# Prompt attention chunkwise inside the V projection, a sigmoid gate, and the sample's state update moved into the output projection

## The reference, cut to what matters

```python
b = cumsum(lf); dmat = b[t] - b[s] + ig[s], -inf where s > t
m = maximum(b + m0, max(dmat))
s = (q @ k.T) * exp(dmat - m)
num = s @ v + exp(b + m0 - m) * (q @ C0)
h = num / maximum(abs(den), exp(-m))
C1 = exp(b[-1] + m0 - m[-1]) * C0 + (a * k).T @ v
y = (rmsnorm(h) * g_head * sigmoid(o)) @ w_out
```

## Time and profile before

| | |
|---|---|
| median of 3 runs | 1549.89 us (1546.93 to 1554.04) |
| profiled execution | 1557.0 us |
| its span | 1554.3 us |
| TensorE busy in the span | 1436.3 us, 92% |
| VectorE, ScalarE, GpSimd busy | 48%, 26%, 35% |
| TensorE's mean granted clock | 0.932 of 2.4 GHz |

### The profile page before, as it was taken

How to read it: one execution, slowest core, us unless ns; L and a number is a source line. 1 busy time by engine, 2 the same in 40 slices (tenths; PEclk the granted TensorE clock), 3 DMA queues, 4 the chain that set the end, 5 groups by cost and what they waited for, 6 DMA issues and landing times.

```text
span 1554.3 us, 28123 instructions
## 1 busy us (share of the span) xinstructions
PE 1436.3 (92%) x11820; PEld 1379.3 (89%) x11820; DVE 744.6 (48%) x1062; ACT 401.9 (26%) x641; POOL 538.4 (35%) x282
## 2 busy tenths in 40 slices
PE   5798998779798998999999979999979999999996
PEld 4687996558798998998999979999979999999996
DVE  3621166547347324324315761495875264462673
ACT  2422221025223222222222223222232222222222
POOL 1223341125332332332334424443423444444430
PEclk8698998859898999999999979999979999999997
DMA  9566541270562563563463312232312333223312
GB/s 275 171 124 152 161 125 41 78 45 1 142 168 83 149 184 106 146 187 111 138 190 86 94 55 82 82 96 84 92 45 82 95 88 87 83 78 96 94 55 58
DMA packets 328027, 167.45 MB, mean 108 GB/s; under 512 B 16159, under 2 KB 326119, under 8 KB 327794
## 3 DMA queue, kind: packets, MB, share of 16 engines
q1 hardware_dynamic: 241426, 121.07, 29.9%
q10 hardware_dynamic: 86336, 44.77, 10.5%
q0 software_dynamic: 160, 0.07, 0.0%
HBM read 158.97 MB, written 6.91 MB: 107 GB/s over the span
## 4 chain that ended last, share of the span: by engine, by line
PE 66%; issue 14%; POOL 6%; DVE 6%; SPq 4%; DMA 1%; ACT 1%; ACTq 0%; POOLq 0%; DVEq 0%
PE G L1247 42%; PE G L1269 14%; POOL wl L664 6%; SPq L301 2%; PE B L1526 2%; PE G L1504 2%; PE B L1287 1%; PE B L1468 1%; DMA raw<-in_mlstm_w_in 1%; SPq L336 1%; PE B L1297 1%; DVE small_s L1201 1%; PE B L1233 1%; DVE yc L1200 1%; PE B L1496 1%
## 5 line engine op out<-in xcount | busy, mean ns | idle before, releaser
L664 POOL TENSOR_TENSOR wl<-raw,wh 128x1024 fp32r<-128x1024 f32 x192 | 479.8, 2502 | 770.0 <-ACT wh L401 769.9
L1247 PE MATMUL G<-Xh,wh 128*128 128x272 f32 x1536 | 326.1, 294 | 0.0
L1247 PE MATMUL G<-Xl,wh 128*128 128x272 f32 x1536 | 319.5, 289 | 0.0
L1247 PE MATMUL G<-Xh,wl 128*128 128x272 f32 x1536 | 317.8, 288 | 0.0
L408 ACT ACTIVATE stage<-G 128x544 f32<-128x544 f32 x168 | 105.0, 625 | 687.5 <-PE G L1247 543.1
L1247 PEld LDWEIGHTS G<-Xh,wh 128*128 128x128 f32 x1536 | 241.7, 190 | 14.3 <-issue 14.3
L401 ACT ACTIVATE wh<-raw 128x1024 fp32r<-128x1024 f32 x192 | 202.4, 1054 | 197.0 <-PE G L1269 72.6
L1247 PEld LDWEIGHTS G<-Xl,wh 128*128 128x128 f32 x1536 | 243.7, 190 | 0.0
L1247 PEld LDWEIGHTS G<-Xh,wl 128*128 128x128 f32 x1536 | 242.6, 190 | 0.0
L810 DVE SCALAR_TENSOR_TENSOR xT<-stage,modT,xT 128x512 f32<-128x512 f32 x80 | 75.5, 944 | 308.9 <-ACT stage L408 287.1
L1247 PE MATMUL G<-Hh,wh 128*128 128x272 f32 x864 | 180.3, 290 | 0.0
(11 more groups left out here) (238 smaller groups left out, 1580.5 us busy)
## 6 DMA issues: line engine op xcount, KB each, us to landing
aring<-in_ada_w ACTq DMA_DIRECT2D x80, 512.0 KB, 5.1
raw<-in_mlp_w_up SPq DMA_DIRECT2D x64, 512.0 KB, 4.1
raw<-in_mlp_w_down SPq DMA_DIRECT2D x64, 512.0 KB, 3.9
raw<-in_mlstm_w_in SPq DMA_DIRECT2D x24, 512.0 KB, 3.8
raw<-in_conv_w_in SPq DMA_DIRECT2D x24, 512.0 KB, 3.8
early<-in_ada_w SPq DMA_DIRECT2D x16, 512.0 KB, 7.4
raw<-in_mlstm_w_out SPq DMA_DIRECT2D x8, 512.0 KB, 6.6
raw<-in_conv_w_out SPq DMA_DIRECT2D x8, 512.0 KB, 3.9
```

The lines of the kernel that those rows point to most:

```text
L664: nc.gpsimd.tensor_tensor(wl[:, t % SLOTS], raw[:, t % RAWS], wh[:, t % SLOTS].bitcast(F32), ALU.subtract).then_inc(s_lo, 1)
L1247: last = mm(G[:, 2 * (g % 2) + hf, 0:HALF], w[:, s, k, :], x[:, k, hf * HALF:(hf + 1) * HALF], start=st, stop=en)
```

## The change

Prompt attention goes by chunks of 128 tokens. A head now has only the four diagonal blocks of scores, four key-value products, a state carried over the chunks by VectorE (`states`), and per chunk after the first a product of decayed queries with the state. Its steps stand between the contraction steps of the V tile after its own (`head`), and at the end of that tile (`head_product`); head 7 stands in O tile 0. The prompt's state falls out of the last chunk, and SP stores it during O. The samples' rows are spread by small products on TensorE in place of the way through DRAM. The V projection has no modulation pairs; each later projection of layer 0 takes the set of the one before, and the first MLP's last quarter takes the last set. The gate is ScalarE's Sigmoid. The samples' old-state products and attention stand within O tiles, their state update within output-projection tiles 2 to 5, with one VectorE instruction for each of 32. SP's order: three V weights, the sample's state, the other V weights and four of O, the prompt state's stores, the rest of O; then, after the samples' rows are done (`s_ys`), x and all weights of the output projection; then the sample state's stores; then the MLP's. The first MLP's loop makes two passes, and the first and last quarters are written out.

```diff
-STATE_TILE = 4
+STATE_TILE = 2
@@ SyncE @@
+unit(T_V, w_in, D, order=range(3))
...
-unit(T_V, w_in, D)
-unit(T_O, w_in, 2 * D)
-unit(T_WOUT, w_out, 0, order=range(3))
+unit(T_V, w_in, D, order=range(3, KT))
+unit(T_O, w_in, 2 * D, order=range(4))
+sp.wait_ge(s_st, H)
+for h2 in range(2):
+    mine = Cfin[DK * h2:DK * (h2 + 1), :, :]
...
+unit(T_O, w_in, 2 * D, order=range(4, KT))
+sp.wait_ge(s_ys, 1)
+sp.wait_ge(s_out, 16 * 4)
+for k in range(KT):
+    nc.sync.dma_start(xT[:, k, :], xspill[:, k * TOK:(k + 1) * TOK]).then_inc(s_back, 16)
+unit(T_WOUT, w_out, 0)
 sp.wait_ge(s_cud, 1)
...
-sp.wait_ge(s_y, H)
-sp.wait_ge(s_num, H)
-for k in range(KT):
-    nc.sync.dma_start(xT[:, k, :], xspill[:, k * TOK:(k + 1) * TOK]).then_inc(s_back, 16)
-unit(T_WOUT, w_out, 0, order=range(3, KT))
...
@@ ScalarE @@
+    for i in range(NJ):
+        c = slice(i * P, (i + 1) * P)
+        last = nc.scalar.activation(dexp[h % 2][:, c], B4[:, c], ACT.Exp, bias=tok[:, 0, i, h:h + 1])
+    last.then_inc(s_d, 1)
...
+for m in range(KT):
+    if m >= 1:
+        decays(m - 1)
+    hi(T_V + m + LEAD)
+    if m >= 2:
+        turned_out(m - 2)
+    to_v(T_V + m, G_V + m, None, 0, 0)
+    if m >= 1:
+        head_out(m - 1)
...
+to_gate = to_stage(ACT.Sigmoid)
...
+    hi(T_O + m + LEAD)
...
+    to_gate(T_O + m, G_O + m, None, 0, 0)
...
@@ GpSimd @@
+def mask(h):
+    pool.wait_ge(s_d, h + 1)
+    blocks = dexp[h % 2][:, :].rearrange("p (j c) -> p j c", j=NJ)
+    nc.gpsimd.affine_select(out=blocks, in_=blocks, compare_op=ALU.is_ge, fill=0.0, base=0,
+                            pattern=[[0, NJ], [1, P]], channel_multiplier=-1).then_inc(s_sel, 1)
+def head_power(h):
+    pool.wait_ge(s_sq, h + 1)
+    nc.gpsimd.tensor_tensor(stat[:, 3, :], stat[:, 2, :], mhalf[:, 0:NJ], ALU.pow).then_inc(s_rs, 1)
...
+for h in range(-1, H):
+    if h >= 1:
+        head_power(h - 1)
+    if h >= 0:
+        mask(h)
+    lo(T_V + LEAD + h + 1)
@@ VectorE @@
+def scaled_queries(a):
+    if a:
+        dve.wait_ge(s_pv, 2 * a)
+    V.tensor_copy(decs[:, :], B6[:, P - 1:SEQ - P:P])
+    V.tensor_tensor(qt[:, :], qT[:, a, P:SEQ], B6[:, 0:SEQ - P], ALU.mult).then_inc(s_qe, 1)
+def weights(h):
+    dve.wait_ge(s_s, h + 1)
+    dve.wait_ge(s_sel, h + 1)
+    V.scalar_tensor_tensor(dexp[h % 2][:, :], B5[:, :], KS, dexp[h % 2][:, :], ALU.mult, ALU.mult).then_inc(s_pr, 1)
+def states(h):
+    pr = slice(DK * (h % 2), DK * (h % 2) + DK)
+    dve.wait_ge(s_u, h + 1)
+    dve.wait_ge(s_qe, h // 2 + 1)
+    if h >= 2:
+        dve.wait_ge(s_pv, h - 1)
+    chain.link(V.tensor_copy(Sst[pr, 0, :], B7[pr, 0:DVA]))
+    for i in range(1, NJ - 1):
+        chain.link(V.scalar_tensor_tensor(Sst[pr, i, :], Sst[pr, i - 1, :], decs[pr, i - 1:i],
+                                          B7[pr, i * DVA:(i + 1) * DVA], ALU.mult, ALU.add))
+    V.scalar_tensor_tensor(Cfin[pr, h // 2, :], Sst[pr, NJ - 2, :], decs[pr, NJ - 2:NJ - 1], B6[pr, 0:DVA],
+                           ALU.mult, ALU.add).then_inc(s_st, 1)
...
+for h in range(H):
+    if h:
+        head_factor(h - 1)
+    values(h)
+    if h % 2 == 0:
+        scaled_queries(h // 2)
+    if h:
+        head_done(h - 1)
+    weights(h)
+    states(h)
...
+mixer_residual = residual(2, 1)
+for m in range(KT):
+    mixer_residual(m, G_WOUT + m, None, 0)
+    if STATE_TILE - 1 <= m < STATE_TILE - 1 + H // 2:
+        update_state(m - STATE_TILE + 1)
@@ TensorE @@
+def head(h):
+    a, pr = h // 2, slice(DK * (h % 2), DK * (h % 2) + DK)
+    def between(k):
+        if k == 0:
+            if h >= 2:
+                pe.wait_ge(s_hc, h - 1)
+            elif h == 0:
+                pe.wait_ge(s_ktd, 4)
+            mm(B4[:, :], sel[:, h, :], negMp[:, :], start=True, stop=True).then_inc(s_bc, 1)
+        if k == 1:
+            if h:
+                pe.wait_ge(s_pr, h)
+            else:
+                pe.wait_ge(s_sp, 1)
+            for i in range(NJ):
+                c = slice(i * P, (i + 1) * P)
+                last = mm(B5[:, c], kT[pr, a, c], qT[pr, a, c], start=True, stop=True)
+            last.then_inc(s_s, 1)
+        if k == 2:
+            pe.wait_ge(s_ev, G_V + h + 1)
+            if h:
+                pe.wait_ge(s_num, h)
+            st_ = stage[(G_V + h) % 2]
+            for jt in range(NJ):
+                turn(B7[:, jt * P:(jt + 1) * P], st_[:, col(jt * P):col(jt * P) + P], P)
+            last = turn(B6[0:NS, SEQ - P:SEQ], vs[(G_V + h) % 2][:, :], P)
+            if h % 2 == 0:
+                last = mm(B6[:, 0:SEQ - P], selp[:, a, :], erow[:, :], start=True, stop=True)
+            last.then_inc(s_vt, 1)
+        if k == 5:
+            pe.wait_ge(s_dr, G_V + h + 1)
+            pe.wait_ge(s_qe, a + 1)
+            for i in range(NJ):
+                out = B7[pr, i * DVA:(i + 1) * DVA] if i < NJ - 1 else B6[pr, 0:DVA]
+                last = mm(out, ktok[:, i, h * DK:(h + 1) * DK], vtok[:, i, h, :], start=True, stop=True,
+                          tile_position=(0, DK * (h % 2)))
+            last.then_inc(s_u, 1)
+        if k == 6 and h:
+            pe.wait_ge(s_d, h + 1)
+            turn_head(h - 1)
+    return between
+def head_product(h):
+    a, pr = h // 2, slice(DK * (h % 2), DK * (h % 2) + DK)
+    pe.wait_ge(s_pr, h + 1)
+    pe.wait_ge(s_st, h + 1)
+    for jt in range(NJ):
+        out = (B7, B6)[jt // 2][:, (jt % 2) * DVA:(jt % 2 + 1) * DVA]
+        last = mm(out, dexp[h % 2][:, jt * P:(jt + 1) * P], vtok[:, jt, h, :], start=True, stop=(jt == 0))
+        if jt:
+            last = mm(out, qt[pr, (jt - 1) * P:jt * P], Sst[pr, jt - 1, :], start=False, stop=True)
+    last.then_inc(s_pv, 1)
+for m in range(KT):
+    tile(T_V + m, G_V + m, Xh, Xl, None, 0, 0, head(m - 1) if m else before_heads)
+    if m:
+        head_product(m - 1)
...
+O_STEPS = {(1, 5): lambda: turn_head(H - 1), (3, 1): sample_numerators, (5, 1): sample_turned}
...
+for m in range(KT):
+    tile(T_O + m, G_O + m, Xh, Xl, None, 0, 0, gate_steps(m) if m else head(H - 1))
+    if m == 0:
+        head_product(H - 1)
+    if m == 1:
+        sample_scores()
+    if m == 2:
+        pe.wait_ge(s_hc, H)
+    if m in ADA_AFTER_O:
+        ada_pair(4 * 3 + ADA_AFTER_O[m])
+pe.wait_ge(s_ys, 1)
+ada_turn(3)
...
-            mm((B5, B7)[n % 2][:, 0:2 * DVA], kam[a % 2][:, b, :],
-               vtok_s[:, 2 * a:2 * a + 2, :].rearrange("p h e -> p (h e)"), start=True, stop=True).then_inc(s_cu, 1)
+            for h2 in range(2):
+                last = mm((B5, B7)[n % 2][DK * h2:DK * (h2 + 1), 0:DVA], kam[a % 2][:, b, DK * h2:DK * (h2 + 1)],
+                          vtok_s[:, 2 * a + h2, :], start=True, stop=True, tile_position=(0, DK * h2))
+            last.then_inc(s_cu, 1)
...
+mixed(T_WOUT, G_WOUT, 4, Yh, Yl, x_ready(X_Y), between=state_products)
...
-with pe.Fori(0, QUARTERS - 1) as j:
-    mixed(T_MLP0, G_MLP0, 6, Xh, Xl, MLP0_X, j, 16, 16, 2)
-    mixed(T_MLP0 + 8, G_MLP0 + 8, 7, Hh, Hl, drained(G_MLP0, j, 16), j, 16, 16, 2)
-unit(T_MLP0_LAST, G_MLP0_LAST, Xh, Xl, ready=MLP0_X)
+mixed(T_MLP0, G_MLP0, 5, Xh, Xl, MLP0_X)
+mixed(T_MLP0 + 8, G_MLP0 + 8, 6, Hh, Hl, drained(G_MLP0))
+with pe.Fori(0, QUARTERS - 2) as j:
+    mixed(T_MLP0L, G_MLP0L, 7, Xh, Xl, MLP0_X, j, 16, 16, 2)
+    mixed(T_MLP0L + 8, G_MLP0L + 8, 8, Hh, Hl, drained(G_MLP0L, j, 16), j, 16, 16, 2)
+mixed(T_MLP0_LAST, G_MLP0_LAST, 11, Xh, Xl, MLP0_X)
```

More of the change, by code:

```diff
@@ L534, in rows_sample, with maxima_out @@
                 nc.scalar.activation(sample(rows[2][:, :]), sample(rows[2][:, :]), ACT.Exp).then_inc(s_ra, 1)
[L536 to L540 removed]
+            def maxima_out():
                 nc.scalar.dma_start(outs[4][0, 0, :].rearrange("(h o) -> h o", o=1), rows[0][:, LAST_COL:LAST_COL + 1])\
@@ L1098, in head_norm, with norm_heads @@
                 V.tensor_scalar(st[2], st[4], 1.0 / DV, EPS, ALU.mult, ALU.add).then_inc(sq_sem, 1)
-                if meanwhile is not None:
-                    meanwhile()
+            def norm_heads(nm, npart, w, rs_n, hs_out, out_sem):
+                st = [stat[0:npart, i, 0:w] for i in range(5)]
                 dve.wait_ge(s_rs, rs_n)
@@ new lines, in _ @@
+            head_factor(H - 1)
+            head_done(H - 1)
+            gated(0)
+            dve.wait_ge(s_srs, 5)
+            chain.link(V.tensor_tensor(qe[:, :, :], qs[:, :, :], einter_s[:, :, :], ALU.mult))
+            for h2 in range(2):
+                pr = slice(DK * h2, DK * (h2 + 1))
+                for b in range(SB):
+                    last = V.tensor_copy(qbd[pr, :, b, NS * h2 + ST * b:NS * h2 + ST * (b + 1)], qe[pr, :, ST * b:ST * (b + 1)])
+            last.then_inc(s_sp, 1)
@@ new lines, in _ @@
+            gated(1)
+            dve.wait_ge(s_ssc, 1)
+            for h2 in range(2):
+                pick = lambda ap: ap.rearrange("p (a h) t -> p a h t", h=2)[:, :, h2, :]
+                last = V.scalar_tensor_tensor(
+                    pick(probs_s[:, :, :])[:, :, NS * h2:NS * (h2 + 1)],
```

(21 more changed lines are left out.)

676 lines of the change are left out of this document (289 added, 387 removed).

## The result

| | before | after |
|---|---|---|
| median of 4 runs | 1550.56 us (1546.93 to 1554.04) | 1574.27 us (1563.21 to 1587.37) |
| ratio after to before | | 1.0119, 95% interval 1.0082 to 1.0156 |
| profiled execution, span | 1557.0, 1554.3 us | 1565.4, 1563.8 us |
| mean granted clock | 0.932 | 0.932 |

One of the four runs of after, 1587.37 us, counts as slow and is left out of the ratio; the median of the other three is 1565.4 us.

The account below looks back on a forecast made before the run. Matmuls bound V, O and output projection; keys, gap and attention left TensorE idle. Terms -12.4 + 44.9 - 121.6 + 57.3 - 0.5 = -32.3 us, median 1549.9 to 1517.6; 8-in-10 range 1487 to 1546.

Parts of the forecast that it names:

- Step 1: Query and key tiles: stall behind the state's loads goes, half of 11.6 us idle kept; 62.4 against 74.8, -12.4 us.
- Step 2: V with seven heads: tile 0 at 12.2, seven tiles at 13.3; 105.3 against 60.4, +44.9 us.
- seven products at 0.243: End of each tile with a head: seven products on TensorE, 1.7 us of the head's 6.2 us.
- Rivals B and C: V tiles: B, heads' hand-over becomes the bound, 1567 us, chance 0.08; C, nothing of a head hides, 1550, chance 0.09.
- Step 3: O, gap and attention: 81.8 against 203.4, -121.6 us, including +8.2 waiting for x's reload and W_out.
- Step 4: Output projection: 65.6 us to last update, then 44.9 behind 18 stores; 110.5 against 53.2, +57.3, of it 30.5 stall.
- About 1 us for VectorE behind its residual: Output projection: allowance for VectorE's residual within the 65.6 us to the last update.
- Rival D: V tiles: VectorE's scaling waits for GpSimd's whole weight split, 2.4 us a tile, 19 us over eight; 1537, chance 0.10.
- the landing, "6.5": Output projection: first MLP weight lands 6.5 us after the 18 store issues, which take 23.3 us.
- 5 us later behind the small pieces: Output projection: upper bound, stall 36 us instead of 30.5 if the MLP weight lands 5 us later.
- Step 5: MLPs: one pass less of the first loop -6.2, one modulation set +5.7, second loop without gaps; -0.5 us.
- Rival A: Output projection: stores do not hold the weights, TensorE loses little or nothing; 1487 us, half of it 1502, chance 0.23.

Follow-up runs that it names:

- the padded kernels: Kernels with satisfied waits added at TensorE's program start; on the changed kernel alone, 128 gave span 1556.9 us and 64 gave 1564.6; on the kernel before, 128 gave 1548.6.
- the kernel with all edits together: Changed kernel plus three MLP weights before the stores, GpSimd held back in the output projection, head products grouped, 128 satisfied waits: 1507.6 us, ratio to before 0.973.

## Why the prediction was wrong

The forecast's sum against the trace, by its own steps (us, profiled execution):

| step | forecast | measured | what made the difference |
|---|---|---|---|
| 1 query and key tiles | 62.4 | 56.3 | no wait at all: the idle time kept for the pair's load did not come |
| 2 V | 105.3 | 113.7 | tile 0 1.2 less; a tile with a head 0.8 more, seven times; 3.0 of half clock in one tile; 1.1 in the first head's tile |
| 3 O | 81.8 | 87.9 | 2.7 waiting for the samples' weights, the rest small |
| 4 projection to last update | 65.6 | 77.1 | VectorE waits for GpSimd, then half clock |
| 4 last update to end | 44.9 | 54.8 | the weight lands after 19.3, not 6.5 |
| 5 MLPs and rest | -0.5 | +11.5 | loop returns in the second MLP |

**Step 1 and step 3's removal** held: keys came out 18.5 us shorter against 12.4, and attention's and the gap's 106 us are gone from TensorE. The half of the old idle time, 5.8 us, that the sum kept for the pair's load did not come.

**Step 2**: the tile's breaks were right. An even tile's other work is 6.7 us and the matmuls with their breaks are 6.8, where the forecast had 6.2 and 7.05. The term mis-sized is "seven products at 0.243", taken from ten products of one kind in a row; alternating kinds cost 0.42. Rivals B and C, a V tile bound by the hand-over, fell: TensorE waited 0.4 us in all of V.

**Step 3**: the wait for the reload and W_out was sized well (6.6 us and a cold tile, for 8.2), but its stated cause is incomplete: with the weights early, the modulation load took their place.

**Step 4** failed twice, and a term that was too high hid part of it by luck. "About 1 us for VectorE behind its residual" took VectorE's durations as they stand alone. Rival D had the mechanism and put it in V, where the order of a tile keeps split and scaling apart; there it did not occur (scalings took 0.7 to 1.2 us). It occurred where splits and residuals meet by design, and cost 20.3 us (77.1 less the 56.8 without it), of which the waits are under 5 and the half clock behind them the rest. Nothing in the sum let a short wait of TensorE switch its clock for 38 us, although O had shown it before. Only 11.5 of the 20.3 stand in the table, because the sum was 8.8 too high for a projection at full clock: it took 0.80 for each of 32 state products from the earlier trace rows, a product of 258 columns. The change makes two of 129 columns, each into its own half of the output rows, and they take 0.37 together instead of 0.63: six matmuls and a product are 1.31 us and not 1.58, 8.6 us in all. For the stores, the issues (23.3, measured 20.8), the way to the last tile and its cold clock were right, and the landing, "6.5", was not. That row stands behind the state's loads, whose 18 issues alone took 27.1 us; behind the stores the issues were done sooner and the landing was late, 40.1 us in all. Without the two stores of single floats the landing is 4.8: it was these that the sum did not price. The bound "5 us later behind the small pieces" had the cause and was too small by 8.

**Step 5** failed by the part that it declared settled: "the second MLP's loop returns without a gap". The sentence on the Trainium skill's page "Runtime: NRT & Kernel Launch", section "Instruction fetch mechanics", should have been read the other way round. It says that a taken branch out of the window stalls; that the second loop did not stall before could be a property of where it lay, which the change moved. The trace of after and the padded kernels agree with that, though none shows the fetch itself, and the page was set aside for one row that could change.

Rival A, 1487 us, was wrong for the stores as they are. For the 16 large ones alone it would have been half right: without the others the last update and the projection's end lie 30.9 us apart, 16.5 us of stall where the forecast had 30.5 and A none. The range's upper end, 1546, covered D and left out C; it did not cover a loss of D's kind, a longer landing and loop returns together. The stretches together miss the forecast by 41.8 us: 11.5 and 9.9 in the output projection, 12.0 in the MLPs, 8.4 in V and 6.1 in O, less 6.1 in the key tiles.

## What to carry to other kernels

When work is moved under a matmul stream, list for every VectorE instruction with two SBUF inputs which GpSimd instruction can start before it; price it at its own length plus all of theirs, and price a TensorE wait behind it with the half clock that may follow. Keep stores in single floats away from any load that something waits for, by fetching that load well ahead; and look at what every queue fetches behind them. After a change to a long program compare also the loops that were not touched: their returns can begin or stop to cost, and a few idle waits can decide it.

## What was not expected of the hardware

- The clock can fall with TensorE busy all the time. In V of after, with no idle time in the eleven microseconds ahead of it, and 0.4 us before those:

```profile
155.00:160.00 5.00, 5.00 (x22) 4.52 (x22) 0.04 (x1) 1.48 (x4) 3.94 (x3) 0.50 0.00 0
160.00:165.00 5.00, 5.00 (x36) 4.62 (x35) 2.89 (x8) 0.00 (x0) 0.00 (x0) 0.89 0.36 105
```

  It costs 3 us there. It is not the program: of the kernels whose V is that of after, some have it, mostly at another place, and three have none (without the single floats, with them behind two weights, and with 64 waits). In the kernel with all edits together V has none either (113.0 us busy of 113.0, clock 1.00). Its cause stays open.
- A wait of 3.7 us before small products was followed by 38 us of half clock in one execution and over 70 in another, and a wait of 1.9 us by 14; the same products without the wait kept 1.00.
- Two state products of 129 columns into two halves of the output rows take 0.37 us together, where one of 258 columns took 0.63, both at full clock.
- Two stores of 16 KB together, written in single floats, delay the next load by 14.5 us (19.3 for 4.8).
- 128 idle waits at the start of TensorE's program removed 12 us from its last loop in one kernel, and nothing in another that had no gap there.
